# Last unit of an output projection in pieces of 384 and 128 columns, with its addition and its square divided alike

## What is computed

```python
def rmsnorm(x, w):
    y = xf * lax.rsqrt(jnp.mean(xf * xf, axis=-1, keepdims=True) + EPS)
    return (y * w).astype(x.dtype)

x = x + _even_layer(x, ...)      # ends with concat(ya, yb) @ w_out     (e_out)
x = x + _odd_layer(x, ...)       # ends with (o * silu(gate)) @ w_out   (o_out)
x = rmsnorm(x, final_norm)       # then the second block:
x = x + mixer(rmsnorm(x))        #                                      (g_out)
x = x + memory_xattn(rmsnorm(x)) # ends with o @ w_o                    (x_out)
x = x + conv_ffn(rmsnorm(x))     # ends with (silu(gate) * up) @ w_down (f_down)
out = rmsnorm(x, final_norm_2)
```

## Time and profile before

| | |
|---|---|
| median of 3 runs | 2405.45 us (2403.34, 2405.45, 2405.47) |
| the profiled execution | 2403.0 us, its span 2401.3 us |
| PE busy | 2383.2 us, 99% of the span |
| PEld, DVE, ACT, POOL busy | 2066.5, 1630.6, 1174.5, 158.0 us |
| mean granted TensorE clock | 0.999 of full speed |

### The profile page before, as it was taken

One profiled execution on the slowest core, in us unless ns is written; L12 is line 12 of the kernel. 1 busy time (PEld: TensorE's weight loads), 2 busy tenths in 40 slices (PEclk: granted clock), 3 DMA queues, 4 the chain that ended last, 5 costly groups with the idle time before them and its releaser, 6 DMA issues.

```text
span 2401.3 us, 35487 instructions
## 1 busy us (share of the span) xinstructions
PE 2383.2 (99%) x14097; PEld 2066.5 (86%) x14097; DVE 1630.6 (68%) x2076; ACT 1174.5 (49%) x1434; POOL 158.0 (7%) x142
## 2 busy tenths in 40 slices
PE   8999999999999999999999999999999999999998
PEld 7888988898888888889988888988888888888887
DVE  6999776555685876696655446666776467755764
ACT  5443674544565654642654345545554334433433
POOL 1000000000200100000000000000212012200220
PEclk9999999999999999999999999999999999999999
DMA  8555546455435555653175555445665556555554
GB/s 252 192 194 186 165 140 212 151 187 164 158 110 206 175 175 177 193 158 106 39 257 178 194 188 163 143 173 173 192 195 181 204 176 200 183 200 186 185 179 143
DMA packets 337350, 422.45 MB, mean 176 GB/s; under 512 B 8494, under 2 KB 263228, under 8 KB 336716
## 3 DMA queue, kind: packets, MB, share of 16 engines
q1 hardware_dynamic: 334220, 410.87, 52.0%
q0 software_dynamic: 2544, 8.52, 1.1%
q10 hardware_dynamic: 464, 1.32, 0.2%
HBM read 418.53 MB, written 2.10 MB: 175 GB/s over the span
## 4 chain that ended last, share of the span: by engine, by line
PE 98%; DVE 1%; ACT 1%; DMA 0%; issue 0%; ACTq 0%
PE ps L779 37%; PE ps L780 19%; PE ps L836 10%; PE ps L837 10%; PE ps L838 10%; PE ps L782 1%; PE ps L784 1%; PE ps L783 1%; PE ps L1150 1%; PE ps L1142 1%; PE ps L1063 1%; PE ps L1067 1%; PE ps L1090 0%; DMA x<-in_x 0%; PE ps L875 0%; PE ps L889 0%
## 5 line engine op out<-in xcount | busy, mean ns | idle before, releaser
L779 PE MATMUL ps<-h_cat,w_hi 128*128 128x512 f32 x3824 | 1340.6, 395 | 1.8 <-DVE h_cat L2378 1.2
L780 PE MATMUL ps<-h_cat,w_lo 128*128 128x256 f32 x3824 | 1066.3, 279 | 0.0
L779 PEld LDWEIGHTS ps<-h_cat,w_hi 128*128 128x128 f32 x3824 | 716.4, 187 | 169.5 <-issue 5.3
L780 PEld LDWEIGHTS ps<-h_cat,w_lo 128*128 128x128 f32 x3824 | 720.7, 188 | 2.1 <-issue 1.9
L2234 DVE TENSOR_TENSOR w_lo<-ring,w_hi 128x2048 fp32r<-128x2048 f32 (+2 forms) x279 | 588.4, 2111 | 163.6 <-ACT w_hi L1454 161.1
L1454 ACT ACTIVATE w_hi<-ring 128x2048 fp32r<-128x2048 f32 (+2 forms) x279 | 493.3, 1769 | 89.4 <-PE ps L838 64.4
L2230 DVE TENSOR_TENSOR w_lo<-ring,w_hi 128x2048 fp32r<-128x2048 f32 (+1 forms) x136 | 302.9, 2233 | 229.3 <-ACT w_hi L1451 226.4
L1451 ACT ACTIVATE w_hi<-ring 128x2048 fp32r<-128x2048 f32 (+1 forms) x136 | 252.2, 1862 | 270.2 <-PE ps L838 244.4
L1472 ACT ACTIVATE stage<-ps 128x256 f32<-128x256 f32 x144 | 55.4, 384 | 398.9 <-PE ps L780 398.8
L836 PE MATMUL ps<-w_hi,h_cat 128*128 128x512 f32 x640 | 250.0, 391 | 0.0
L838 PE MATMUL ps<-w_hi,h_cat 128*128 128x512 f32 x640 | 249.2, 389 | 0.0
(11 more groups left out here) (471 smaller groups left out, 2325.8 us busy)
## 6 DMA issues: line engine op xcount, KB each, us to landing
ring<-in_w_ffn_up SPq DMA_DIRECT2D x44, 2048.0 KB, 8.0
ring<-in_w_mix_in SPq DMA_DIRECT2D x28, 2048.0 KB, 8.3
ring<-in_even_w_in SPq DMA_DIRECT2D x27, 2048.0 KB, 8.1
ring<-in_w_ffn_down SPq DMA_DIRECT2D x16, 2048.0 KB, 8.0
ring<-in_odd_w_in SPq DMA_DIRECT2D x11, 2048.0 KB, 9.4
ring<-in_even_w_out SPq DMA_DIRECT2D x8, 2048.0 KB, 8.2
ring<-in_odd_w_out SPq DMA_DIRECT2D x8, 2048.0 KB, 8.9
ring<-in_w_mix_out SPq DMA_DIRECT2D x8, 2048.0 KB, 8.1
```

Of the source, the lines that this page charges most:

```text
L779: mm(o[:, 0:2 * T], whi[slot][:, k, :], flat(cat[:, k]), start=first, stop=False)
L780: ins = mm(o[:, T:2 * T], wlo[slot][:, k, :], cat[:, k, 0, :], start=False, stop=end)
```

## The change

The last unit's second token half becomes two runs: all k tiles for 384 columns into the old bank, then all for 128 columns into columns 0 to 127 of another bank (`side`), which is free by then: the accumulator bank of the segment behind, or ps0 for f_down2. DVE adds 384 columns when the first run is done (`most_ready`), then what the earlier three units left in the old bank's other 128 columns, and last the 128 columns of the second run. ACT squares 384 and then 128 columns, the latter with its result going to the side bank and its sum to `part_last`; DVE adds the first sum to the running one (`add_most`) and the root takes the second. The constant matmuls go to the second half of ps6, with 256 columns fewer behind e_out and x_out and 128 fewer behind o_out. The counts of `based` follow.

```diff
+    part_last = place("part_last", [P, 1])
...
+    MOST = 3 * P
+    ENDS = {"e_out": 0, "o_out": 1, "x_out": 2, "f_down2": 3}
+    def side(name):
+        return ps[0] if name == "f_down2" else acc[{g.name: BEHIND[k] for k, g in IN_FRONT.items()}[name].f0 % ACC]
...
                 for t in range(TT):
-                    for j in range(g.units - 4, g.units):
+                    for j in range(g.units - 4, g.units - t):
                         wide_unit(g, j, h_cat if cat is None else cat, tiles_ready, act0, (t,), tile=tile)
+                end_unit(g, h_cat if cat is None else cat, tile)
...
+        def end_unit(g, cat, tile):
+            n, o, apart_ = g.n0 + g.units - 1, pair(g, 3)[1], side(g.name)
+            slot, toks = n % WHL, slice(P, 2 * P)
+            before = seg_of_narrow[(BEHIND_OF[g.name].f0 if g.name in BEHIND_OF else len(seg_of_narrow)) - ACC]
+            pe.wait_ge(sem["lo_ready"], n + 1)
+            pe.wait_ge(*emptied(before[0], before[1] + 1))
+            for cols, to in ((slice(0, MOST), o[:, 0:MOST]), (slice(MOST, WIDE), apart_[:, 0:WIDE - MOST])):
+                for kk in range(g.kq):
+                    k = (3 * g.kq + kk + g.k0) % g.kt
+                    first, end = cols.start > 0 and kk == 0, kk == g.kq - 1
+                    hi, lo = quarter(whi[slot], g, kk)[:, cols], quarter(wlo[slot], g, kk)[:, cols]
+                    rows_of = cat[:, k] if tile is None else tile(k)
+                    mm(to, rows_of[:, 0, toks], hi, start=first, stop=False)
+                    mm(to, rows_of[:, 0, toks], lo, start=False, stop=False)
+                    ins = mm(to, rows_of[:, 1, toks], hi, start=False, stop=end)
+                ins.then_inc(sem["acc_ready" if cols.start else "most_ready"], 1)
...
-                for cols in {1: (T, P), 2: (T, T, T), 5: (T, P)}[norm]:
-                    mm(bank(behind, behind.n0)[:, 0:cols], ident[:], causal[:, 0:cols], start=True, stop=True)
+                for cols in {1: (P,), 2: (T, T, P), 5: (P,)}[norm]:
+                    mm(ps[6][:, T:T + cols], ident[:], causal[:, 0:cols], start=True, stop=True)
...
         def square_row(g, t):
...
+            act.wait_ge(sem["most_added"], ENDS[g.name] + 1)
+            if st["squared"] >= 2:
+                act.wait_ge(sem["squared"], st["squared"] - 1)
+            most = slice(3 * WIDE, 3 * WIDE + MOST)
+            af(dump[:, st["squared"] % 2, 0:MOST], x[:, 1, most], ACT.Square, scale=D ** -0.5,
+               accum_out=part[:, 0, 1, 3:4]).then_inc(sem["squared"], 1)
+            st["squared"] += 1
+            act.wait_ge(sem["last_added"], ENDS[g.name] + 1)
+            af(side(g.name)[:, P:2 * P], x[:, 1, 3 * WIDE + MOST:], ACT.Square, scale=D ** -0.5,
+               accum_out=part_last[:]).then_inc(sem["last_squared"], 1)
...
         def root_of(t, based, std, which=0, last=0):
             act.wait_ge(sem["squared"], st["squared"])
             act.wait_ge(sem["based"], based)
-            af(root[:, 0, t:t + 1], part[:, which, t, 3:4], ACT.Sqrt, bias=so_far[:, which, t:t + 1]).then_inc(sem[std], 1)
+            piece = part[:, which, t, 3:4]
+            if t == 1 and which == 0:
+                act.wait_ge(sem["last_squared"], last)
+                piece = part_last[:]
+            af(root[:, 0, t:t + 1], piece, ACT.Sqrt, bias=so_far[:, which, t:t + 1]).then_inc(sem[std], 1)
...
         def add_row(g, t):
...
+            dve.wait_ge(sem["most_ready"], ENDS[g.name] + 1)
+            o, v = pair(g, 3)[1], x[:, 1, 3 * WIDE:]
+            tt(v[:, 0:MOST], v[:, 0:MOST], o[:, 0:MOST], ALU.add).then_inc(sem["most_added"], 1)
+            tt(v[:, MOST:], v[:, MOST:], o[:, MOST:], ALU.add).then_inc(sem["emptied"], 1)
+            dve.wait_ge(sem["acc_ready"], g.n0 + 16)
+            dve.wait_ge(sem["emptied"], 2 * (g.w0 + 3) + 2)
+            tt(v[:, MOST:], v[:, MOST:], side(g.name)[:, 0:WIDE - MOST], ALU.add).then_inc(sem["last_added"], 1)
+
+        def add_most(squared):
+            dve.wait_ge(sem["squared"], squared)
+            return tt(so_far[:, 0, 1:2], so_far[:, 0, 1:2], part[:, 0, 1, 3:4], ALU.add)
...
             add_row(g, 1)
+            add_most(SQUARES[k]).then_inc(sem["based"], 1)
             inverse_of(1, "std_ready", roots).then_inc(sem["rstd_ready"], 1)
...
         def two_norms(t, squared, std, rstd, count):
+            else:
+                ch.link(add_most(squared))
+                dve.wait_ge(sem["last_squared"], ENDS["o_out"] + 1)
+                ch.link(tt(first, part_last[:], so_far[:, 0, t:t + 1], ALU.add))
...
         add_row(S["o_out"], 1)
-        dve.wait_ge(sem["emptied"], 2 * S["o_out"].w0 + 8)
+        dve.wait_ge(sem["last_added"], ENDS["o_out"] + 1)
         tt(last_row, two_of(last), two_of(gain1[:, 3 * WIDE:]), ALU.mult).then_inc(sem["gained"], 1)
```

More of the change, by code:

```diff
@@ L408, in build @@
              "hi_ready", "lo_ready", "acc_ready", "drained", "summed", "gated", "posted",
-             "row_ready", "emptied", "squared", "gained", "totalled", "std_ready", "rstd_ready", "scaled_dve", "scaled_act", "turned",
+             "row_ready", "most_ready", "most_added", "last_added", "last_squared", "emptied", "squared", "gained", "totalled", "std_ready", "rstd_ready", "scaled_dve", "scaled_act", "turned",
              "scaled_one", "based", "half_std", "half_rstd", "ht_hi", "ht_ready", "tiles_read", "agate_read", "hhi_ready", "h_ready", "x_normed", "gain1_loaded", "gain_out_loaded",
@@ L720, in two_of @@
         return v.rearrange("p (a t) -> p a t", a=2)
+    BEHIND_OF = {g.name: BEHIND[k] for k, g in IN_FRONT.items()}
+    MOST = 3 * P
+    ENDS = {"e_out": 0, "o_out": 1, "x_out": 2, "f_down2": 3}
+    def side(name):
+        return ps[0] if name == "f_down2" else acc[{g.name: BEHIND[k] for k, g in IN_FRONT.items()}[name].f0 % ACC]
     def xs_of(norm, c, t):
@@ L1627, in square_row, with root_of @@
         def square_row(g, t):
-            act.wait_ge(sem["emptied"], 2 * (g.w0 + 3) + t + 1)
-            square(x[:, t, 3 * WIDE:], 0, t, 3)
-        def root_of(t, based, std, which=0):
+            if t == 0:
+                act.wait_ge(sem["emptied"], 2 * (g.w0 + 3) + 1)
+                square(x[:, 0, 3 * WIDE:], 0, 0, 3)
+                return
+            act.wait_ge(sem["most_added"], ENDS[g.name] + 1)
[8 more added lines that the diff above has]
+               accum_out=part_last[:]).then_inc(sem["last_squared"], 1)
+        def root_of(t, based, std, which=0, last=0):
             act.wait_ge(sem["squared"], st["squared"])
             act.wait_ge(sem["based"], based)
-            af(root[:, 0, t:t + 1], part[:, which, t, 3:4], ACT.Sqrt, bias=so_far[:, which, t:t + 1]).then_inc(sem[std], 1)
+            piece = part[:, which, t, 3:4]
[3 more added lines that the diff above has]
+            af(root[:, 0, t:t + 1], piece, ACT.Sqrt, bias=so_far[:, which, t:t + 1]).then_inc(sem[std], 1)
         def halved_rows(k, roots, free, source):
@@ L1653, in halved_norm @@
             square_row(g, 1)
-            root_of(1, based, "std_ready")
+            root_of(1, based + 1, "std_ready", last=ENDS[g.name] + 1)
             halved_rows(k, roots, g, row_of(x, 1))
@@ L1897, in _ @@
         square(x[:, 0, 3 * WIDE:], 1, 0, 3)
-        root_of(0, 3, "half_std", 1)
+        root_of(0, 4, "half_std", 1)
         split_to(S["g_qkv"].n0 + 3)
@@ L1902, in _ @@
         square(last_row, 1, 1, 3)
-        root_of(1, 4, "std_ready", 1)
+        root_of(1, 5, "std_ready", 1)
         halved_rows(2, 3, S["o_out"], row_of(x, 1))
@@ L2171, in _ @@
         wide_seg("x_out", lambda c: squares(S["x_out"], c))
-        halved_norm(5, 7, 5, S["x_out"], "f_up0")
+        halved_norm(5, 7, 6, S["x_out"], "f_up0")
         for p in range(3):
@@ L2201, in _ @@
         square_row(S["f_down2"], 0)
-        root_of(0, 6, "half_std")
+        root_of(0, 8, "half_std")
         square_row(S["f_down2"], 1)
-        root_of(1, 6, "std_ready")
+        root_of(1, 9, "std_ready", last=4)
         act.wait_ge(sem["rstd_ready"], 8)
@@ L2398, in add_row @@
                 dve.wait_ge(sem["row_ready"], g.w0 + 4)
[L2399 to L2402, removed]
+                v = x[:, 0, 3 * WIDE:]
+                tt(v, v, pair(g, 3)[0][:], ALU.add).then_inc(sem["emptied"], 1)
+                return
+            dve.wait_ge(sem["most_ready"], ENDS[g.name] + 1)
[8 more added lines that the diff above has]
+            return tt(so_far[:, 0, 1:2], so_far[:, 0, 1:2], part[:, 0, 1, 3:4], ALU.add)
         def base(squared, which=0):
@@ L2753, in two_norms @@
         def two_norms(t, squared, std, rstd, count):
-            dve.wait_ge(sem["squared"], squared)
             first = root[:, 1, t:t + 1]
-            ch.link(tt(first, part[:, 0, t, 3:4], so_far[:, 0, t:t + 1], ALU.add))
+            if t == 0:
+                dve.wait_ge(sem["squared"], squared)
+                ch.link(tt(first, part[:, 0, t, 3:4], so_far[:, 0, t:t + 1], ALU.add))
+            else:
```

(4 more changed lines are left out.)

## The result

| | before | after |
|---|---|---|
| median | 2403.63 us (2403.01 to 2405.47, 7 runs) | 2414.19 us (2410.54 to 2415.79, 7 runs) |
| ratio after to before | | 1.004, 95% interval 1.003 to 1.0049 |
| profiled execution | 2403.0 us, span 2401.3 | 2415.64 us, span 2413.9 |

The change made the kernel slower by 10.6 us, outside the range of the prediction (2402.5 to 2408.0) and beyond its slowest rival (2410.4). Later runs of the kernel before gave medians of 2403.2 to 2403.6.

The account below looks back on a forecast made before the run. TensorE matmul time was taken as the bound, busy 2383.2 of 2401.3 us. Terms -0.03 (e_out), -0.03 (x_out), +0.28 (o_out), -0.20 (f_down2) sum to +0.02 us, leaving the median at 2405.4 us; range 2402.5 to 2408.0.

Parts of the forecast that it names:

- The change touches these four places and no other: Only the final VectorE adds behind e_out, o_out, x_out and f_down2 were said to change, in all +0.02 us.
- Slower: Outcome slower by at least the measurable 4.8 us, needing rival b's upper end or rival c; chance 0.09.
- No more than about 2.4 us: At each place, the most time said to stand between last matmul and dependent transpose, mostly filled by necessary transposes.
- The pace of 128 columns: Second run of the split last unit: 0.111 us a matmul, set by weight loads, so 12 take 1.33 us.
- rival a: At the four places, 128-column matmuls run at 0.067 us because loads hide: -1.4 us, 2404.1 us; chance 0.10.
- rival b: At the four places, rounded 128-column matmuls are as slow as plain fp32, 0.22 us: +5.0 us, 2410.4; chance 0.17.
- rival c: TensorE's clock falls; 4.8 us would need 3.2 us at 1.2 GHz at each of three places; chance 0.03.
- The adds: VectorE at each place: 0.553 us for 384 columns, hidden, and 0.283 for the last 128, saving 0.405.
- The square: ScalarE's last square, 128 instead of 512 columns: 0.32 us, saving 0.31, at least 0.23.
- o_out: Gain multiplication becomes the second square's wait, so the place costs +0.28 us; z to dependent transpose 6.34 us.
- f_down2: At the kernel's end: +0.52 TensorE, -0.405 add, -0.31 square, giving -0.20 us.
- Constants: Fewer constant filler matmuls behind e_out, x_out and o_out were said to cost nothing and give nothing.

Follow-up runs that it names:

- the unused 32 bytes: Kernel before the change plus an unused 4-byte tile (32 with padding) where the change puts part_last: 2413.89 us, ratio 1.004; second time 2413.86 us.
- two tiles put back: Kernel before plus the unused 32-byte tile, with act_cat (and the four tiles behind it) and gate_cat back at a multiple of 256 from w_hi: 2405.67 us, 1.0006.
- 64 bytes: Kernel before the change plus an unused tile of 64 bytes at part_last's place, moving all tiles behind it: 2415.42 us, ratio 1.0051.

## Why the prediction was wrong, step by step

- **"The change touches these four places and no other"** is the step that failed. The prediction costed instructions and waits, and left out what a new 4-byte tile does to the addresses of all tiles behind it. The runs measured +10.3 us for that alone, with the change's instructions absent (2413.89 against 2403.64), and +0.3 us for the instructions without the move (2403.90 against 2403.59). Of the 10.3 us, 1056 x 6.6 ns = 7.0 us are f_down's (6.8 us when `act_cat` moves alone), and some 1.2 us are the 192 matmuls of o_out that read `gate_cat` (227.1 to 233.2 ns). About 2 us are left, and the narrow segments are the place for them: in the profile of the unused 32 bytes, an execution of 2414.87 us, e_v starts 3.3 us late (201.81 against 198.47). That two tiles put back leave a median of +2.1 us fits, but its interval holds zero, so this part is not settled. Also open is why 64 bytes gave 2415.42 us in the median; the one profile of that kernel is of 2412.00 us and has e_val to e_q at their old pace.
- **Range and chances.** The forecast of the sum, +0.02 us, was near to what the change's own instructions do (+0.2 us by the profile, ratios of 1.0001 and 0.9999). The range was too narrow since it held only costs at the places. "Slower" had 0.09, and for other reasons. The forecast also stood on a median of three runs, 2405.45, where later ones of the same kernel gave 2403.2 to 2403.6; on those, "as it is" would have been 2403.6.
- **The stalls.** "No more than about 2.4 us" between the last matmul and the dependent transpose holds at e_out (459.98 - 457.53). At o_out the rows give 787.69 - 784.52 = 3.17 us. No term of the sum uses it.
- **The pace of 128 columns**, 0.111 taken from the weight loads of L1179: measured 0.112. Only the second of them follows the first after 0.06. The line's 0.067 (rival a) and the plain fp32's 0.22 (rival b) are both out, and so are the 81 ns that the Trainium skill gives for 128 columns ("TensorE: Matmul & The Clock Gate", section "Back-to-back issue gap").
- **384 columns**: 2.10 us for 12, forecast 2.08. **The adds**: 0.56, 0.28 and 0.29, forecast 0.553 and 0.283.
- **The square** was mis-sized: its record is 0.28, but square to root is 0.52, forecast 0.44. The accumulator is read from 0.22 to 0.41 behind the square's start, and the root starts 0.11 behind that, where it was 0.03 before. That saves 0.23, the least that the prediction allowed. This is why e_out reads 5.37 and not 5.30.
- **o_out**: 6.34 forecast, 6.34 measured, with the gain multiplication as the wait. **f_down2**: -0.20 forecast, -0.14 measured.
- **Constants**: the wait before the transpose is still ended by DVE's xs, as forecast; fewer of them cost nothing. **The clock** (rival c): 1.00 at all four places. Before the end of PE's work it fell only near 15 us, where the change does nothing, in one profile of the change and in that of the kernel with the two tiles put back, and in no other.

The Trainium skill ("SBUF — State Buffer", section "Who interferes with whom") lists two independent read ports for PE, one for the moving operand and one for weight loads. The 233.3 against 226.8 ns with only the distance of the two operands changed do not fit a picture in which the two reads never meet. What makes them meet was not measured, so a conflict between them is argued here; what is shown is that the pace depends on the distance.

## What to carry to other kernels

In a kernel bound by PE, look at the placement of the matmul operands when a tile is added, however small: put it last, or in spare bytes, or pad it so that stationary and moving operands stay a multiple of 256 bytes apart, as far as it was tried here: fp32r operands and 512 moving columns. When an edit costs more than its instructions can, line up the two traces matmul by matmul and look where the distance between them grows; an unused tile of the same size tells in one run whether the placement did it. And when the tail of a product is split, look at what the last piece costs PE: here a matmul of 128 columns takes 0.112 us and one of 256 takes 0.120, so the smaller piece saves PE next to nothing. A split into 256 and 256 was not tried.

## What the hardware showed that I had not expected

- The distance of stationary and moving operand in SBUF sets the pace of fp32r matmuls of 512 columns: 226.7 to 226.8 ns at multiples of 256 bytes, 232.4 at 128 beside one, 233.3 at 32 or 64 beside one. Moving both together by 128 changes nothing. The slow pace is there with all other engines and DMA idle too, and the records of the weight loads keep their 185 to 186 ns.
- Pairs of 512 and 256 columns have several stable paces within a segment, 346.7 ns or some 353 for the pair, at a granted clock of 1.00 and with PE at 100% busy. Which one a segment takes can differ between two executions of the same kernel: x_k had 353 in one profile of the change and 346.7 in the other.
- A matmul of 128 fp32r columns with its own weight load takes 0.112 us, the pace of the weight loads of L1179 (0.1125 us).
